# High and low weights of the dense matmuls placed 48 bytes further up in their tensors

## What is computed

```python
def first_block(x, p, ...):
    h = x
    for i in range(2):
        xn = rms_norm(h, norm_mix[i])
        mix = hawk_block(xn, ...) if i == 0 else rwkv7_time_mix(xn, ...)
        h = h + mix
        h = h + swiglu(rms_norm(h, norm_ffn[i]), ffn_w_in[i], ffn_w_out[i])
        ple = (p[i] @ ple_w_proj[i]) * sigmoid(rms_norm(h, norm_ple[i]) @ ple_w_gate[i])
        h = h + ple
    return rms_norm(h, norm_final)

def second_block(x, p, ...):
    proj = rms_norm(x, pre_norm_g) @ w_in
    u_ssm, z_ssm, q, k, v, z_attn = split(proj)
    ssm_out = s5_branch(u_ssm, ...) * silu(z_ssm)
    attn_out = swa_branch(q, k, v, attn_sinks) * silu(z_attn)
    h = x + rms_norm(concat(ssm_out, attn_out) @ w_out, post_norm_g)
    return h + sigmoid(h @ pl_w_gate + pl_b_gate) * (p @ pl_w_proj)
```

## Time and profile before

| | us |
|---|---|
| median of 3 executions | 3548.92 |
| lowest, highest | 3545.87, 3551.94 |
| the profiled execution's own time | 3547.82 |
| its span, first to last instruction | 3546.0 |
| PE busy | 3405.1 |
| PEld busy | 2748.4 |
| DVE busy | 1984.6 |
| POOL busy | 1590.5 |
| ACT busy | 1194.9 |

### The profile page before, as it was taken

One profiled execution on the slowest core, in us unless ns is written; L12 is line 12 of the kernel. 1 busy time (PEld: TensorE's weight loads), 2 busy tenths in 40 slices (PEclk: granted clock), 3 DMA queues, 4 the chain that ended last, 5 costly groups with the idle time before them and its releaser, 6 DMA issues. The chain is left out here.

```text
span 3546.0 us, 61071 instructions
## 1 busy us (share of the span) xinstructions
PE 3405.1 (96%) x25028; PEld 2748.4 (78%) x25028; DVE 1984.6 (56%) x2398; ACT 1194.9 (34%) x1597; POOL 1590.5 (45%) x1148
## 2 busy tenths in 40 slices
PE   7998999999999999999999999999999999999989
PEld 5886778888888777888787877888888887674767
DVE  6886565556224652226767647555542458868452
ACT  4654233333102362226465524333310231242221
POOL 3442377775333323334344425877633323560352
PEclk9998999999999999999999999999999999999999
DMA  2111122224311142241212211222332113111212
GB/s 103 48 49 38 33 87 79 80 89 152 109 42 56 40 179 95 95 147 39 85 46 86 68 37 48 88 89 78 111 128 88 52 42 119 61 48 42 101 43 76
DMA packets 74063, 274.58 MB, mean 77 GB/s; under 512 B 8208, under 2 KB 8592, under 8 KB 73360
## 3 DMA queue, kind: packets, MB, share of 16 engines
q1 hardware_dynamic: 68112, 250.79, 20.8%
q10 hardware_dynamic: 5760, 20.97, 1.5%
HBM read 207.77 MB, written 63.96 MB: 77 GB/s over the span
## 5 line engine op out<-in xcount | busy, mean ns | idle before, releaser
L117 POOL TENSOR_TENSOR gap<-ones 128x1 f32<-128x1 f32 x150 | 46.0, 307 | 1238.8 <-PE ps L167 774.4
L120 POOL TENSOR_TENSOR wlo<-wraw,whi 128x1024 fp32r<-128x1024 f32 (+3 forms) x150 | 391.6, 2611 | 12.5
L893 DVE TENSOR_TENSOR h<-ps,h 128x1024 f32<-128x1024 f32 (+1 forms) x56 | 68.5, 1223 | 288.9 <-PE ps L416 259.6
L167 PE MATMUL ps<-xh,whi 128*128 128x512 f32 x640 | 203.0, 399 | 21.6 <-ACT rw_stage L1888 5.1
L167 PE MATMUL ps<-xl,whi 128*128 128x512 f32 x640 | 199.2, 393 | 0.0
L167 PE MATMUL ps<-xh,wlo 128*128 128x512 f32 x640 | 198.7, 392 | 0.0
L1007 POOL TENSOR_TENSOR wlo<-wraw,whi 128x512 fp32r<-128x512 f32 x126 | 166.3, 1335 | 52.6 <-ACT whi L1130 52.6
L118 POOL TENSOR_SCALAR whi<-wraw 128x1024 fp32r<-128x1024 f32 (+3 forms) x150 | 178.9, 1192 | 0.0
L384 ACT ACTIVATE sq<-h 128x1024 f32<-128x1024 f32 x32 | 34.0, 1061 | 394.1 <-DVE h L893 304.0
L2200 POOL TENSOR_TENSOR rw_levels<-rw_levels,rw_masks 128x512 f32<-128x512 f32 x64 | 87.2, 1378 | 177.2 <-PE ps L2289 140.8
L167 PEld LDWEIGHTS ps<-xh,whi 128*128 128x128 f32 x640 | 119.7, 190 | 56.6 <-issue 8.9
(11 more groups left out here) (673 smaller groups left out, 9535.0 us busy)
## 6 DMA issues: line engine op xcount, KB each, us to landing
wraw<-w_ffn_in SPq DMA_DIRECT2D x88, 512.0 KB, 3.5
ffn_hidden<-sum_of_squares SPq DMA_DIRECT2D x44, 512.0 KB, 2.6
rw_next<-rw_kept SPq DMA_DIRECT2D x40, 512.0 KB, 5.1
wraw<-w_ffn_out SPq DMA_DIRECT2D x32, 512.0 KB, 3.6
ffn_stage<-ffn_hidden SPq DMA_DIRECT2D x30, 512.0 KB, 4.9
rw_kept<-rw_stage SPq DMA_DIRECT2D x24, 512.0 KB, 2.7
rw_kept<-rw_stage ACTq DMA_DIRECT2D x24, 512.0 KB, 2.7
wraw<-w_ple SPq DMA_DIRECT2D x16, 640.0 KB, 3.8
```

The source lines that it names most:

```text
L117: nc.gpsimd.tensor_tensor(g.gap[:, 0:1], g.ones[:, 0:1], g.ones[:, 0:1], ALU.mult)
L120: nc.gpsimd.tensor_tensor(g.wlo[:, s, 0:w], g.wraw[:, s, 0:w], g.whi[:, s, 0:w].bitcast(F32), ALU.subtract).then_inc(g.w_split.sem, 1)
L167: last = nc.tensor.matmul(acc[:, hf, :], w[:, s, c:c + P], x[:, kt, hf * HALF:(hf + 1) * HALF], start=start and kt == 0 and n == 0, stop=s ...
L893: nc.vector.tensor_tensor(ht, flat(banks(g, acc + 2 * s)), ht, ALU.add).then_inc(g.acc_free.sem, 1)
```

## The change

whi and wlo are allocated with 16 more elements (64 bytes) per partition, and the kernel uses a view that begins 12 elements (48 bytes) inside. whi then starts at byte 47,760 and wlo at 58,064, both 16 modulo 64. What is allocated behind them moves by 128 bytes (the arena to 72,416) and stays where it was modulo 64. The row tensors, at 32 modulo 64, so lie 16 bytes behind the weights modulo 64; ffn_wh and ffn_wl stay at 32.

```diff
@@ build
         g.gap = ctx.enter_context(nc.sbuf_tensor("gap", [P, 2], F32))
-        g.whi = ctx.enter_context(nc.sbuf_tensor("whi", [P, 2, WMAX], F32R))
-        g.wlo = ctx.enter_context(nc.sbuf_tensor("wlo", [P, 2, WMAX], F32R))
+        W_LEAD = 12
+        whi = ctx.enter_context(nc.sbuf_tensor("whi", [P, 2 * WMAX + 16], F32R))
+        wlo = ctx.enter_context(nc.sbuf_tensor("wlo", [P, 2 * WMAX + 16], F32R))
+        g.whi, g.wlo = (w[:, W_LEAD:W_LEAD + 2 * WMAX].rearrange("p (s c) -> p s c", s=2) for w in (whi, wlo))
         g.sumsq = ctx.enter_context(nc.sbuf_tensor("sum_of_squares", [P, T], F32))
```

## The result

The changed kernel takes 3594.03 us (median of 4 runs, 3591.56 to 3595.08) against 3550.43 us of the kernel before (median of 4, 3545.87 to 3556.33): the ratio is 1.0121, with a 95% interval of 1.0103 to 1.0138. It is slower by 43.6 us. The forecast was 3522 us and faster, and the measured time lies 2 us above the upper end of the range (3592 us). The rival that comes nearest is the slower one (3590 us, +4 ns for each matmul).

What follows compares the result with a forecast made beforehand. TensorE's start-to-start matmul spacing was taken as the bound: 10,160 matmuls times -2.7 ns gave -27 us, writers and other engines zero, so 3548.9 us became 3522 us; the 8-in-10 range was 3445 to 3592 us.

Steps and rivals of the forecast that it cites:

- 10,160 matmuls: 96% of the 10,584 matmuls reading whi or wlo, counted as passing any difference to the end; 10.2 us per nanosecond.
- The controls that the prediction named: Predicted unmoved: ffn_wh/ffn_wl matmuls at 226.7 ns, half-clock spacing at 426 ns, bf16 run at 215.8 ns, writers' rows.
- I take a quarter of the floor's gain: Step sizing the spacing change of whi/wlo matmuls: -2.7 ns each, -27 us in all; called the weakest step.
- the 10.9 ns: Excess of the fp32r spacing, 226.7 ns, over the bf16 run's 215.8 ns; removing all of it would give -111 us.
- several meetings: Weight load and row stream meet a fixed number of times per load; the shift removes the first, 2.7 ns.
- the upper bound: Spacing after a stall, 232 ns, as the most a whi/wlo matmul could lengthen: +5.3 ns, +54 us.
- part (2): Address step: rows minus weights modulo 64 goes from 0 to 16 for 10,584 matmuls, stays 0 for 1512.
- the change doesn't do what it says: Rival: a tensor behind whi and wlo slipped by something other than a multiple of 64; excluded, no chance given.
- The slower rival: Equal places modulo 64 are favourable; whi/wlo matmuls lengthen by +4 ns, +41 us, to 3590 us; chance 0.24.
- Its picture: Slower rival's mechanism: set 16 bytes apart, the faster row stream catches up with the place the load is using.

Runs made afterwards that it cites:

- pure form: Kernel before with whi and wlo each 64 elements longer and both weights 48 bytes up, nothing else moved modulo 256: 3602.47 us, ratio 1.015.
- the probes: Kernel before plus groups of identical extra matmuls at chosen weight and row places, read for distances between starts; fp32r 512 columns: 226.6 to 236.7 ns.
- lead 60: Kernel before with whi and wlo each 64 elements longer and both weights begun 60 elements in: 3551.55 us, ratio 1.0008.
- the grid: Kernel before plus 256 groups of 22 fp32r matmuls, weights and rows each shifted 0 to 240 bytes in 16s: steady means 226.6 to 236.7 ns.
- null: Kernel before with whi and wlo each 64 elements (256 bytes) longer and no lead: 3551.4 us, ratio 1.0003.
- both +32: Kernel before with whi and wlo 64 elements longer, lead of 8 and 8 elements ahead of the rows, moving weights and rows 32 bytes: 3549.5 us.
- lead 44: Kernel before with whi and wlo each 64 elements longer and both weights begun 44 elements in: 3573.55 us, ratio 1.0056.
- low 16: Kernel before with whi and wlo each 64 elements longer, high weights at lead 0, low weights at lead 60: 3553.41 us, ratio 1.0.
- high alone: Kernel before with whi 32 elements longer and only the high weights moved by 48 bytes: 3574.23 us, ratio 1.0075.
- lead 16: Changed kernel with a lead of 16 elements (64 bytes) instead of 12: 3573.58 us, ratio 1.0052 to the kernel before.
- lead 8: Changed kernel with a lead of 8 elements (32 bytes) instead of 12: 3588.86 us, ratio 1.0107 to the kernel before.
- low alone: Kernel before with low weights moved 48 bytes inside a wlo 32 elements longer, which also moved the rows 128 bytes: 3594.11 us, ratio 1.013.
- lead 32: Kernel before with both weights moved by 32 elements: high weights 128 bytes, low weights and rows 256 bytes: 3600.33 us, ratio 1.0139.

## Why the prediction was wrong

**Right: what bounds the kernel, and who passes a difference on.** The sum was 10,160 matmuls times one difference. The difference turned out as +4.6 ns: 47 us, and measured are 43.6 us. By the busy times it is 47.2 us of TensorE's work with whi and wlo, 4.7 us of which fell into waits. The controls that the prediction named all held: ffn weights, half clock, bf16, writers. That 96% of the matmuls pass the difference on is a little too much where it is larger: in the pure form (lead 12) 6.4 ns x 10,160 = 65 us, and 50.7 us were measured, since TensorE's waits shrank by 12.1 us there.

**Wrong, and decisive: the step that sized the difference, "I take a quarter of the floor's gain" (-2.7 ns).** It started from equal places modulo 64 as the cause of the 10.9 ns and let 16 bytes take away the first of several meetings. The runs show the opposite sign, +4.6 ns. Equal places are at the floor (226.7 ns, at weights on a multiple of 32 bytes), and the 10.9 ns are not meetings that a shift can remove, since none of 256 places is below 226.6 ns. The fp32r matmul has an extra of 13.3 ns even there. The prediction had called this its weakest step, and it had the row that spoke against it: after a stall the same operands run at 232 ns and then come back to 226.7. That the spacing returns to its shorter value by itself was the only evidence on another state of these matmuls in the whole trace, and it pointed up. I used it as the upper bound and took the value from an argument instead of from the row. One reading of these rows was wrong as well: the weight load does not stand "differently against the running matmul" there. In the trace of the kernel before it starts 2 to 4 ns after the stream in the long distances as in the short ones. So it stays open what differs after a stall, and that the sign was the same there is no proof of one cause.

**Wrong: part (2), the places.** "Rows minus weights is 0 before and 16 after" is true modulo 64 and beside the point. The unit is 256 bytes (the probes, and the kernels with leads of 16 and 32 elements, which are equal modulo 64 or 128 and slower). With it, the 64 bytes by which each tensor grew are part of the change: 80 and 16 bytes instead of 16 and 16. The rival "the change doesn't do what it says" was excluded with the argument that all moves are multiples of 64. That was an argument inside the assumed unit.

**The slower rival** was right in its direction: the position of the kernel before is a favourable one. That its +4 ns came near the 4.6 ns is luck. It was meant for rows 16 bytes behind both weights, and the kernel with just that modulo 256 (lead 60) has 227.6 ns, 0.7 more than before; the 4.6 ns are those of 80 and 16 bytes in two patterns. Its picture, one read catching up with the other, was only argued and is not shown by any run. The upper end of the range took in 3592 us, just under the time: it was drawn from +4 ns, while the earlier trace rows bounded the case at +5.3 ns, which makes 3549 + 54 = 3603 us. That bound would have held both the change and its pure form (3602 us).

**The rule from the Trainium skill.** The measured table by stream and next load says that the place of the next weights decides how long the stream takes, by up to 10 ns in 227. Which of two values a place takes can depend on what ran before, too. The Trainium skill, TensorE: Matmul & The Clock Gate, Part 2 (step 1), says that loading the next weights does not take read bandwidth from the running matmul; by that rule this change would have been no change (3549 us), and for bf16 and fp32 operands the probe agrees with it. For fp32r the measurement decides against it. The Trainium skill, SBUF — State Buffer, Specifications, has 16-byte cachelines; shifts by whole lines, which by that rule are neutral, cost up to 10 ns here, and 4 bytes within a line 10 ns.

**How the kernels fit the grid of places.** With one difference for all weights, the grid foretells the kernel's mean distance within 0.3 ns; with two it is off by up to 2.1 ns, to either side:

| kernel | rows behind high, low | by the grid | in the kernel | time, us |
|---|---|---|---|---|
| null | 0, 0 | 226.7 | 226.95 | 3551.4 |
| both +32 | 0, 0 | 226.7 | 227.0 | 3549.5 |
| lead 60 | 16, 16 | 226.7 to 228.3 | 227.6 | 3551.55 |
| lead 44 | 80, 80 | 230.0 | 230.0 | 3573.55 |
| lead 12, pure | 208, 208 | 233.3 | 233.3 | 3602.47 |
| low 16 | 0, 16 | 226.7 | 227.1 | 3553.41 |
| high alone | 80, 0 | 228.9 | 230.2 | 3574.23 |
| lead 16 | 64, 0 | 228.2 | 229.9 | 3573.58 |
| the change | 80, 16 | 229.4 | 231.5 | 3594.03 |
| lead 8 | 96, 32 | 233.3 | 232.1 | 3588.86 |
| low alone | 128, 80 | 232.2 | 232.3 | 3594.11 |
| lead 32 | 128, 0 | 231.4 | 233.3 | 3600.33 |

The grid's value for two differences is the mean weighted by the loads, two of high weights to one of low. The change lies 2.1 ns above it, some 20 us. Its shorter pattern alone, 229.5 ns, is what the grid foretells (229.4 ns); the surplus is the time in the longer one. Why this mixture has a second pattern is not explained. Lead 16 and lead 32 are 1.7 and 1.9 ns above their grid values, lead 8 is 1.2 ns below.

**What stays open.** No run shows what in the memory or in TensorE has the unit of 256 bytes, why an odd multiple of 16 turns some good differences into bad ones, or what selects one of two steady patterns at the same addresses. Reads that meet in the memory are one picture; that the extra does not grow with the columns, nor shrink with narrower loads, speaks against its simple form (a meeting per stretch read). The patterns of four and six distances, and two values at one place, show that how long a matmul takes depends on those before it.

## What to carry to other kernels

In a stream of fp32r matmuls of 512 columns, keep the weights of the *next* matmul and the moving rows at the same place modulo 256 bytes, on a multiple of 32; tensors that begin at the same place and whose sizes are multiples of 256 bytes stay so by themselves. The bf16 and fp32 matmuls tried here did not need it, and with 448 or 256 columns other places were better. Before moving a tensor, write down the places of all its neighbours in several units, since padding one tensor moves all behind it, and run the padding without the shift as a null. Where a prediction needs a price that the trace doesn't show, take the sign from the only rows that show another state of the same thing, here the spacing after a stall, and not from a picture of the mechanism.

## What the hardware showed beside this

- The steady distance of equal fp32r 128x512 matmuls at 2.4 GHz depends on the addresses: 226.6 to 236.7 ns, a spread of 4.5%, with a period of 256 bytes. Not on them alone: weights +16, rows +0 gave 226.7 ns in one probe and 233.3 ns in another.
- In the changed kernel the stream is held up by the place of the load that runs beside it, not by the weights that it uses: 230.9 ns for ffn streams ahead of a moved load, 226.6 ns the other way round. With lead 8 it takes four distances to get back.
- A weight load starts 2 to 4 ns after the stream that it runs beside, whether the distance is 226 or 236 ns.
- Rows at +4 bytes, inside the same 16 bytes, cost 10 ns (236.7 ns); at +8 bytes 6.7 ns.
- 448 columns took 206.7 ns at +0 and 202.2 ns with the weights 48 bytes up: which place is good depends on the number of columns, too.
- At 1.2 GHz the changed kernel shows nothing of it (0.85 us for a pair, as before).
